# The bias of twelve gate products, in one core's two-block layer: from fp32 rows loaded for each job to one stored fp32r tile

## The reference

```python
h = rms_norm_2(x, norm_w[i])
proj = h @ w_in[i]
(g_qkv, g_z, g_b, g_a, r_feat, r_z, s_u, s_z, gate_logits) = _split_cols(proj, SPLIT_SIZES)
...
gates = jax.nn.sigmoid(gate_logits.astype(jnp.float32).reshape(bsz, seq, N_BRANCH, D_MODEL)
                       + gate_b[i].astype(jnp.float32))
merged = jnp.sum(gates * branch_proj, axis=2)
```

## Time and profile before

| | |
|---|---|
| median of 3 runs | 3671.26 us (3664.84 to 3678.46) |
| the profiled execution's span | 3655.0 us |
| PE busy | 3308.5 us, 91%, 18811 products |
| DVE busy | 2606.1 us, 71% |
| ACT busy | 1266.7 us, 35% |
| POOL busy | 414.2 us, 11% |
| DMA | 870.30 MB, mean 238 GB/s |

### The profile page before, as it was taken

How to read it: one execution, slowest core, us unless ns; L and a number is a source line. 1 busy time by engine, 2 the same in 40 slices (tenths; PEclk the granted TensorE clock), 3 DMA queues, 4 the chain that set the end, 5 groups by cost and what they waited for, 6 DMA issues and landing times. The chain is left out here.

```text
span 3655.0 us, 46514 instructions
## 1 busy us (share of the span) xinstructions
PE 3308.5 (91%) x18811; PEld 2594.7 (71%) x18811; DVE 2606.1 (71%) x3318; ACT 1266.7 (35%) x1467; POOL 414.2 (11%) x393
## 2 busy tenths in 40 slices
PE   7989878989889998999999979898999998999898
PEld 5756646788889998778777768666874674543676
DVE  5856768889999997678788854746446444894664
ACT  3323233334445554444444343312322111100333
POOL 0011101100121221133232100011000110000000
PEclk8889889999999999999999989999999999999899
DMA  9974367847989999899999765223645215442663
GB/s 358 379 274 139 115 224 285 314 167 251 330 322 353 363 362 362 322 371 382 369 376 379 274 205 195 80 76 108 216 162 190 67 31 147 138 154 94 220 222 150
DMA packets 294613, 870.30 MB, mean 238 GB/s; under 512 B 33584, under 2 KB 108436, under 8 KB 242432
## 3 DMA queue, kind: packets, MB, share of 16 engines
q1 hardware_dynamic: 257616, 670.64, 51.7%
q0 software_dynamic: 34320, 190.40, 13.6%
q10 hardware_dynamic: 2464, 6.29, 0.5%
HBM read 820.22 MB, written 46.38 MB: 237 GB/s over the span
## 5 line engine op out<-in xcount | busy, mean ns | idle before, releaser
L2489 DVE TENSOR_TENSOR expert_w_low<-expert_w,expert_w_high 128x2048 fp32r<-128x2048 f32 x256 | 585.5, 2287 | 151.1 <-ACT expert_w_high L2916 148.7
L2824 PE MATMUL bank<-h_halves,expert_w_high 128*128 128x384 f32 x2048 | 610.4, 369 | 61.7 <-DVE expert_w_low L2489 61.5
L2916 ACT ACTIVATE expert_w_high<-expert_w 128x2048 fp32r<-128x2048 f32 x256 | 490.4, 1916 | 443.7 <-DMA expert_w<-in_peer_v_dram 298.8
L294 DVE TENSOR_TENSOR weights_low<-weights,weights_high 128x1024 fp32r<-128x1024 f32 (+4 forms) x288 | 338.2, 1177 | 297.4 <-ACT weights_high L277 294.0
L2825 PE MATMUL bank<-h_halves,expert_w_low 128*128 128x192 f32 x2048 | 519.7, 254 | 0.0
L277 ACT ACTIVATE weights_high<-weights 128x1024 fp32r<-128x1024 f32 (+4 forms) x288 | 293.6, 1022 | 468.3 <-PE bank L322 385.2
L2824 PEld LDWEIGHTS bank<-h_halves,expert_w_high 128*128 128x128 f32 x2048 | 393.3, 192 | 72.5 <-DVE expert_w_low L2489 72.1
L2825 PEld LDWEIGHTS bank<-h_halves,expert_w_low 128*128 128x128 f32 x2048 | 399.6, 195 | 0.0
L2893 PE MATMUL bank<-expert_w_high,gated_acts_halves 128*128 128x512 f32 x512 | 203.0, 396 | 22.4 <-DVE expert_w_low L2489 22.1
L2895 PE MATMUL bank<-expert_w_high,gated_acts_halves 128*128 128x512 f32 x512 | 201.0, 393 | 0.0
L2894 PE MATMUL bank<-expert_w_low,gated_acts_halves 128*128 128x512 f32 x512 | 200.9, 392 | 0.0
(11 more groups left out here) (741 smaller groups left out, 6460.5 us busy)
## 6 DMA issues: line engine op xcount, KB each, us to landing
expert_w<-in_peer_u_dram SPq DMA_DIRECT2D x128, 1024.0 KB
expert_w<-in_peer_v_dram SPq DMA_DIRECT2D x128, 1024.0 KB
weights<-in_ada_w_dram SPq DMA_DIRECT2D x88, 512.0 KB, 9.2
weights<-in_w_out_dram SPq DMA_DIRECT2D x32, 1024.0 KB, 13.3
weights<-in_w_in_dram SPq DMA_DIRECT2D x32, 960.0 KB, 8.7
weights<-in_w_in_dram SPq DMA_DIRECT2D x32, 928.0 KB, 9.8
weights<-in_w_in_dram SPq DMA_DIRECT2D x56, 512.0 KB, 7.3
s_gates_w<-in_w_in_dram SPq DMA_DIRECT2D x56, 512.0 KB, 3.5
```

Of the source, the lines that this page charges most:

```text
L294: dve.tensor_tensor(self.low[:, u % self.UNITS_HELD, :, 0:n], self.buf[b][:, k:k + self.UNIT, 0:n], self.high[:, u % self.UNITS_HELD, :, 0 ...
L2489: dve.tensor_tensor(wl[:, n % RING, :], w_sb[:, n % RING, :], wh[:, n % RING, :], ALU.subtract).then_inc(wl_ready, 1)
L2824: pe.matmul(o[:, 0:2 * DENSE], uh[:, b, k, :], acts.both[:, k, :, 0:DENSE], start=(k == 0), stop=False)
L2916: act.activation(wh[:, n % RING, :], w_sb[:, n % RING, :], ACT.Copy).then_inc(wh_ready, 1)
```

## The change

A new class `GateBias` holds all twelve bias rows in one tile. During the gated delta projection SP loads the twelve rows four times, below one another, into 48 partitions (`raw`). ACT copies them as fp32r into `rows`; DVE then replaces partitions 32 to 47 of `rows` by `raw` minus that copy. So partition j holds the high part of row j, and partition 36 + j the low part. A second tile, `chosen` (48 x 12), has ones at (j, j) and (36 + j, j) and zeros elsewhere, made from the identity. For job j the stationary operand is column j of `chosen`, read 128 times: the product with `rows` gives high plus low of row j for each token.

`on_pe` opens a job's sum with one such fp32r product for each token half, and no longer waits for a load. The bias rows' buffers, semaphores and loads of `Beside` are gone. A job's third field is now the row's number.

```diff
@@ def project(..., bias=None)
+                if bias is not None:
+                    st.gate_bias.on_sp(sp, bias)
...
+                if bias is not None:
+                    st.gate_bias.on_act(act)
...
                         m.weights.split_low(dve, kt, size, source=source if i == 0 else None, between=mod and mod.add_tile)
+                    if bias is not None and i == len(work) - 1:
+                        st.gate_bias.on_dve(dve, st.ident)
...
+class GateBias:
+    N, LOW, COPIES = 12, 32, 4
+    ROWS = N * COPIES
+
+    def __init__(self, m, ctx):
+        self.m = m
+        self.rows = m.sb(ctx, "gate_bias_rows", [self.ROWS, CHUNK], F32R)
+        self.chosen = m.sb(ctx, "gate_bias_chosen", [self.ROWS, self.N], F32R)
+        self.loaded, self.high_ready = m.sem("gate_bias_loaded"), m.sem("gate_bias_high_ready")
+
+    def memory(self, ctx):
+        self.raw = self.m.sb(ctx, "gate_bias_raw", [self.ROWS, CHUNK])
+
+    def choice(self, j):
+        return view(self.chosen[:, j:j + 1], [[0, P]])
+
+    def on_sp(self, sp, bias):
+        src = bias.rearrange("b (c n) -> (b c) n", n=CHUNK)
+        for a in range(self.COPIES):
+            sp.dma_start(self.raw[a * self.N:(a + 1) * self.N, :], src).then_inc(self.loaded, 16)
+
+    def on_act(self, act):
+        act.wait_ge(self.loaded, 16 * self.COPIES)
+        act.activation(self.rows[:, :], self.raw[:, :], ACT.Copy).then_inc(self.high_ready, 1)
+
+    def on_dve(self, dve, ident):
+        low, second = slice(self.LOW, self.ROWS), self.ROWS - self.N
+        dve.tensor_tensor(self.chosen[:, :], ident[0:self.ROWS, 0:self.N], ident[0:self.ROWS, second:self.ROWS], ALU.add)
+        dve.wait_ge(self.high_ready, 1)
+        dve.tensor_tensor(self.rows[low, :], self.raw[low, :], self.rows[low, :], ALU.subtract)
...
 class Beside:
-            if p == 0 and bias is not None:
-                j = self.biased[i]
-                if i >= 2:
-                    sp.wait_ge(self.w_used, self.UNITS * (i - 1))
-                sp.dma_start(self.bias[:, j % 2, :], bias).then_inc(self.b_loaded[j % 2], 16)
...
                 if self.jobs[i][2] is not None:
-                    j = self.biased[i]
-                    pe.wait_ge(self.b_loaded[j % 2], 16 * (j // 2 + 1))
                     for tt in range(TT):
-                        pe.matmul(self.both[tt][:, :], self.st.incl[0:1, :], self.bias[0:1, j % 2, :], start=True, stop=False)
+                        pe.matmul(self.both[tt][:, :], self.st.gate_bias.choice(self.jobs[i][2]), self.st.gate_bias.rows[:, :],
+                                  start=True, stop=False)
```

## The result

The changed kernel runs in 3642.61 us (median of 5 runs, 3638.88 to 3644.65), the kernel before beside it in 3664.84 (5 runs, 3656.17 to 3678.46): a ratio of 0.993, 95% interval 0.991 to 0.995. That is 22.2 us between the medians and 24.6 us by the ratio; the forecast had 19.9.

What follows compares the result with a forecast made beforehand. The prediction took PE, busy 91% of the span, as the bound where gate jobs run. Shorter groups (13.1 us) plus vanished clock falls (6.8 us) gave 19.9 us saved: 3635.1 us of span, 3651.4 us as a run, range 3642 to 3666.

Steps and rivals of the forecast that it cites:

- The group: Bias products opening each gate job on PE: 1.88 us before, 0.62 us after, saving 1.26 us a group.
- The bounds: Saving for one group: 0.72 us if the second load isn't hidden, 1.42 us if the last product gives way early.
- Which groups are on the path: Gate jobs in gated delta, RWKV and S5 stages: ten groups save 1.26 us each, S5's first 0.5; 13.1 us together.
- The set-up: Added loads, ACT copy and DVE operations at the gated delta projection's end: hidden, cost 0; without cover 1.4 us.
- The clock: Four clock falls behind bias groups, 1.70 us each, read as the price of light work: 6.8 us saved, between 0 and 6.8.
- The base: Profiled span 3655.0 us, median of runs shown 3671.3; the 16.3 us between taken as lying around the span.
- the sum's bound of 22.3 us: Upper end of the whole saving: 1.42 x 10 + 1.26 + 6.8 us, giving 3649.0 us.
- The clock still falls: Rival: drain between jobs and change of operands cause the falls, which stay; saving 13.1 us, 3658.2 us; chance 0.22.
- The group isn't that short: Rival: load exposed or fp32r-to-fp32 switch costs; 0.72 us saved a group, 3663.6 us, or 3656.8 without falls; chance 0.11.
- Given back: Rival: PE's gain meets a DVE, ACT or DMA taken for a follower; half the 13.1 us, 3664.7 us; chance 0.08.
- Slower through late set-up: Rival: ACT and DVE wait for the four loads at the gated delta projection's end; 3690 us; chance 0.07.

Runs made afterwards that it cites:

- `long_again`: Changed kernel with each 48-row fp32r product done four times, the same program timed a second time; 3663.11 us, ratio 0.998 to the kernel before.
- `double_light`: Kernel before with each one-row fp32 bias product issued twice, so the bias enters twice; 3703.29 us, ratio 1.010.
- `setup_only`: Kernel before plus the change's set-up alone (four loads, ACT's copy, DVE's two operations), its rows unused; 3669.57 us, ratio 1.001 to the kernel before.
- `fp32_stored`: Changed kernel with the twelve rows loaded once and kept as fp32, no split, fp32 products 12 rows deep; 3667.34 us, ratio 1.000 to the kernel before.
- `deep_fp32`: Stored fp32 rows without split, repeated down all 128 partitions, fp32 products 128 rows deep; timed twice: 3658.25 and 3655.71 us, ratios 0.998 and 0.996 to before.
- `no_bias`: Changed kernel with the bias products left out and the set-up kept; 3639.89 us, ratio 0.993 to the kernel before.

## Why the prediction was right or wrong

*The group.* 1.88 and 0.62 us were forecast; it is 0.62 to 0.66 at all 11 places of the first profile. The bounds weren't needed: with loads of 0.18 us and products of 0.38 us at the least, two of each one after the other would take 1.1 us, so the second load is hidden, and the repeated column adds nothing that shows. Eight 48-row products, each with its load, take 2.01 us in `long_again`, 0.25 us apiece; were a load of 0.18 us (rows 5 have 0.19) paid each time, they could not.

*Which groups are on the path.* 13.1 us were forecast, and the rest of the mean spans fell by 13.1 ± 1.6 us; that the two agree to the tenth is luck, as the spread between the three comparisons shows; `double_light` gives ten groups' worth again. Single places were off by less than a microsecond: the second S5 block's first group now waits 0.8 us for an ACT line that it used to reach later (0.2 before), and from PE's first products to those behind the job, L4525 (now L4555), the first S5 block got 0.9 us shorter, not 0.5.

*The set-up.* Forecast 0, measured 0: by the 6.74 us, and by `setup_only`.

*The clock.* This is the step that failed, in its size. That the falls come with light work and would go was right in these runs (behind 10 of 11 groups in `double_light`, 4 in the kernel before, none of 33 in the changed kernel), with the least behind it; two of its readings were too strong. A fall does stand elsewhere in these jobs: in the first gated delta job 24 passes take 12.16 us from 2348.58, where 24 take 10.57 in the S5 block, at a mean clock of 0.86 and 1.00 (PE waits 2.42 us for DVE soon after, at 2367.31, so it costs nothing). And the two-column products of rows 13 pass without a fall in another execution.

```profile
2348.58 12.16 PE L3245 MATMUL bank<-gdn_gates_w,x_rows 128*128 128x512 f32 x24
...
3115.63 10.57 PE L3245 MATMUL bank<-s_gates_w,x_rows 128*128 128x512 f32 x24
```

The term of the sum that was mis-sized is its 6.8 us. It was four falls times 1.70, read from one execution. The profile of before shows the four: the mean clock of the 4 us that begin 2.4 us after a group's start is 0.57 at the groups of 2404.47, 3203.49 and 3264.94, and 0.63 at that of 2999.24. `setup_only` and `fp32_stored`, with groups of the same length, show six and four; and over all runs the throttle's part is 12.0 ± 1.9 us less (`deep_fp32`, which gives nothing else, 11.3 ± 1.6). The upper bound was put at the 6.8 itself, though a fall came behind only one group in three and another execution could have more. That was the fault: a bound has to hold for executions other than the profiled one. Nor do all falls cost 1.70: `fp32_stored` and `setup_only` each have one of 3.35. Counted so, the falls at groups of this length cost 6.8 us in the profile of before, 8.5 in that of `fp32_stored` and 11.9 in that of `setup_only`, 9.1 ± 1.5 as a mean. The prediction had the lowest of the three. From 9.1 to 12.0 ± 1.9 the distance isn't clear of the noise, and no profile places it.

*The base.* "16.3 us around the span" was wrong. Every run lists its span, and 1.7 to 3.1 us lie around it, 1.9 as a mean. The profiled execution of before was a short one: its clock of 0.949 makes the throttle's part 186 us, against 198 as a mean, while the rest, 3468.6 us, is the mean's. So the gap to the median was mostly clock, and one profile of a clock that varies like that should have been a warning on the 6.8. Little of the gap is the gates' own: ahead of the first gate job the throttle's part is 129.7 us in this profile and 119.5 to 148.5 in the others, 135.9 as a mean, so the executions differ most where no gate job runs. The sum was in effect taken off the median of the three runs shown, 3671.3, which lies 6.4 us above the median beside which the changed kernel was timed. Of the 8.75 us between forecast and result, 6.4 are this, and 2.3 the sum (22.2 by the medians, not 19.9). Five runs are few, though: by the means of all runs, 3667.9 before and 3642.7 after, 3.4 us are the base and 5.3 the sum, which is about what the clock term was short of. The result lies 0.6 us inside the lower end of the range. The lower end of the range had taken in the sum's bound of 22.3 us, but only 7 us for the spread.

*The rivals.* The clock still falls: it doesn't (0 of 33). The group isn't that short: it is. Given back: no, though the S5 block's DVE has only 5.3 us of slack left. Slower through late set-up: the four loads are issued at 2286.46 and their rows used from 2322.95, 36 us later; no run came near it.

How long PE is busy doesn't tell these kernels apart. It is busy through a group of 1.79 us in `deep_fp32` and through one of 1.88 us in the kernel before, with the same 0.26 us of idle time ahead of five of them in the second S5 block; yet the first has 0 falls of 22 and the other 4 of 11, and their mean spans are 3654.5 and 3666.0 us. What differs is the depth of the products, or something that goes with it: the 128 rows also bring more data into each product, and no run holds that apart from depth.

## What to carry to other kernels

A product that is a row or a few deep costs its passes, and in these runs sometimes more behind it: behind 20 of 44 groups of 1.9 to 2.0 us with one row or 12, the granted clock fell to 0.50 for part of the full products that follow, mostly at a cost of 1.70 us. Where such work stands inside a stream on the path, shorten it or give it rows. Groups of 0.63 us and groups with 128 rows had no falls here; 48 rows at the old length still had two in 22. The shorter group is also the one that gives back its own passes. Before a forecast from one profile, set its span and its mean clock beside those of several runs, and take the bound of anything that comes and goes from the number of places where it could have come, not from where it did.

## What the runs showed of the hardware

- Depth: fp32 groups of 1.8 us with 128 rows leave the granted clock at 1.00 behind 22 of 22, groups of 1.88 us with one row or 12 have falls behind 14 of 33. With the form and the length alike, only the rows stored differ between `fp32_stored` (12 rows, 4 of 11) and `deep_fp32` (128 rows, 0 of 22). In both, each column of the stationary operand has one non-zero weight; what the rows that only meet zeros do was not tested by itself.
- Most falls cost 1.70 us here, in five kernels alike: the 64 products behind them take 29.43 us and not 27.73. Others cost 3.35 (one, in `double_light`, 5.0), and all of those begin inside the group: in `double_light` 1.13 us in the group and 2.22 behind it, in `setup_only` 0.39 and 2.96.
- Without light products, 0.26 us of idle time between jobs brought no fall (`no_bias`, 0 of 11).
- Four 512-column fp32 passes differ little with depth: the group is 1.88 us with one row or 12, and 1.79 with 128.
